# Projections of the token mixer: v made turned, low-rank halves side by side, log-gate product as one pass of stacked rows

## The reference

```python
(aq, ak, av, gq, gk, gv, gr, glf, glb, ga, gg) = split_cols(h @ p['w_in'][l])
attn = windowed_gqa(aq..., ak..., av..., p['attn_sink'][l])
...
la_f = log_sigmoid(glf @ p['gla_wa2_fwd'][l] + p['gla_ba_fwd'][l]) / 16
la_b = log_sigmoid(glb @ p['gla_wa2_bwd'][l] + p['gla_ba_bwd'][l]) / 16
```

## Time and profile before

| what | before |
|---|---|
| profiled execution | 3897.49 us |
| span | 3895.8 us |
| granted TensorE clock, mean of the span | 0.951 |
| TensorE busy | 3536.0 us (91%) |
| VectorE busy | 2169.3 us (56%) |
| ScalarE busy | 1593.3 us (41%) |
| GpSimd busy | 651.0 us (17%) |

### The profile page before, as it was taken

How to read it: one execution, slowest core, us unless ns; L and a number is a source line. 1 busy time by engine, 2 the same in 40 slices (tenths; PEclk the granted TensorE clock), 3 DMA queues, 4 the chain that set the end, 5 groups by cost and what they waited for, 6 DMA issues and landing times. The chain is left out here.

```text
span 3895.8 us, 56808 instructions
## 1 busy us (share of the span) xinstructions
PE 3536.0 (91%) x21432; PEld 2934.1 (75%) x21432; DVE 2169.3 (56%) x3920; ACT 1593.3 (41%) x2374; POOL 651.0 (17%) x709
## 2 busy tenths in 40 slices
PE   7699999998889999979999928999999999999991
PEld 3377777766667777757878728999999999999991
DVE  1344534554568888745545465565555555555555
ACT  1344545544334344334444303444444444443442
POOL 0010100101023443402322200011110001000005
PEclk9799999999999999989999858999999999999996
DMA  9733432421754554456555434555555555555567
GB/s 303 238 120 87 136 115 86 130 86 64 232 169 137 168 155 138 120 168 204 187 185 187 154 135 157 157 167 169 170 174 161 165 164 175 172 162 166 162 218 272
DMA packets 544843, 634.46 MB, mean 163 GB/s; under 512 B 77560, under 2 KB 431896, under 8 KB 543776
## 3 DMA queue, kind: packets, MB, share of 16 engines
q1 hardware_dynamic: 506960, 493.72, 40.4%
q0 software_dynamic: 35840, 123.75, 10.0%
q10 hardware_dynamic: 1872, 14.68, 0.9%
HBM read 505.20 MB, written 126.88 MB: 162 GB/s over the span
## 5 line engine op out<-in xcount | busy, mean ns | idle before, releaser
L2414 DVE TENSOR_TENSOR moe_w_lo<-moe_w_raw,moe_w_hi 128x2048 fp32r<-128x2048 f32 x192 | 439.9, 2291 | 371.5 <-ACT moe_w_hi L2362 338.5
L103 PE MATMUL moe_pg<-moe_x_hi,moe_w_hi 128*128 128x320 f32 x2048 | 635.5, 310 | 1.4 <-DVE moe_x_lo L2452 1.4
L104 PE MATMUL moe_pg<-moe_x_lo,moe_w_hi 128*128 128x320 f32 x2048 | 633.8, 309 | 0.0
L105 PE MATMUL moe_pg<-moe_x_hi,moe_w_lo 128*128 128x320 f32 x2048 | 633.8, 309 | 0.0
L2362 ACT CAST moe_w_hi<-moe_w_raw 128x2048 fp32r<-128x2048 f32 x192 | 364.9, 1900 | 158.2 <-DMA moe_w_raw<-in_w_gate_e_dram 81.2
L103 PEld LDWEIGHTS moe_pg<-moe_x_hi,moe_w_hi 128*128 128x128 f32 x2048 | 385.3, 188 | 2.4 <-issue 1.5
L104 PEld LDWEIGHTS moe_pg<-moe_x_lo,moe_w_hi 128*128 128x128 f32 x2048 | 385.4, 188 | 0.6
L105 PEld LDWEIGHTS moe_pg<-moe_x_hi,moe_w_lo 128*128 128x128 f32 x2048 | 385.3, 188 | 0.0
L103 PE MATMUL gla_pd<-gla_h_hi,gla_w_hi 128*128 128x512 f32 x640 | 261.1, 408 | 34.5 <-DVE gla_h_lo L1012 31.9
L103 PE MATMUL pa_pu<-pa_h_hi,pa_w_hi 128*128 128x512 f32 (+1 forms) x560 | 226.9, 405 | 37.4 <-DVE pa_h_lo L644 37.4
L105 PE MATMUL gla_pd<-gla_h_hi,gla_w_lo 128*128 128x512 f32 x640 | 252.4, 394 | 0.0
(11 more groups left out here) (326 smaller groups left out, 7664.0 us busy)
## 6 DMA issues: line engine op xcount, KB each, us to landing
moe_w_raw<-in_w_gate_e_dram SPq DMA_DIRECT2D x64, 1024.0 KB
moe_w_raw<-in_w_up_e_dram SPq DMA_DIRECT2D x64, 1024.0 KB
moe_w_raw<-in_w_down_e_dram SPq DMA_DIRECT2D x64, 1024.0 KB
gla_w_raw<-in_w_in_dram SPq DMA_DIRECT2D x80, 512.0 KB, 4.0
pa_w_raw<-in_w_in_dram SPq DMA_DIRECT2D x35, 1024.0 KB
front_w<-in_w_ada_dram SPq DMA_DIRECT2D x24, 1024.0 KB, 11.9
scratch_gate<-gla_sg POOLq DMA_DIRECT2D x80, 256.0 KB, 2.3
mix_sg<-scratch_gate SPq DMA_DIRECT2D x40, 512.0 KB, 4.6
```

The costliest lines, as they stand in the source:

```text
L103: pe.matmul(out, w_hi, x_hi, start=start, stop=False)
L104: pe.matmul(out, w_hi, x_lo, start=False, stop=False)
L105: return pe.matmul(out, w_lo, x_hi, start=False, stop=stop)
L2414: dve.tensor_tensor(w_lo[:, m % 2], w_raw[:, m % 2], w_hi[:, m % 2].bitcast(F32), ALU.subtract).then_inc(s_wlo, 1)
```

## The change

Three edits, all in `phase_proj_attn`.

1. Unit v is made as k is: its 128 weight columns are stationary and 512 tokens move. ScalarE copies the bank to `vT` (a part of `soft`). A new unit vt after q0 turns it back with four TensorE transposes, and ScalarE copies that bank to `v`.
2. Unit l has high and low weights side by side in `w_hi` as 64 stationary columns. One pass against the high activations gives both products, a second of 32 columns adds high weights x low activations: 16 matmuls instead of 24. The two 32-row halves of the bank are then added: ScalarE copies the one out, VectorE adds the other.
3. The la product is one float32r pass over 96 stacked rows. In `gl` they are high, low, high; in `wa2` high, high, low. ScalarE writes the two high copies, VectorE the low one. The weights are loaded three times (six DMAs instead of two) and split once.

The counts on the semaphore `s_evac` shift by these units (l no longer counts there, vt does), and the waits on the constants go from 80 to 144.

```diff
-BLOCK_UNITS = [("k", 0, 0), ("v", 0, 0), ("q", 0, 1), ("q", 1, 1), ...
+BLOCK_UNITS = [("k", 0, 0), ("v", 0, 0), ("q", 0, 1), ("vt", 0, None), ("q", 1, 1), ...
-ACT_KINDS = ("k", "v", "q", "l", "gq", "gk", "gv")
+ACT_KINDS = ("k", "v", "vt", "q", "gq", "gk", "gv")
...
-        gl = M.sb("gl", [2 * RANK, BLK])
-        wa2 = M.sb("wa2", [2 * RANK, 2, GLA_K])
+        gl = M.sb("gl", [P, BLK], F32R)
+        wa2 = M.sb("wa2", [P, 2, GLA_K], F32R)
+        vT, rank = soft[:, 0], (soft[0:2 * RANK, 1], soft[0:2 * RANK, 2])
+        wa_raw = soft[:, 3].rearrange("p (d n) -> p d n", d=2)
...
-                sp.dma_start(wa2[0:RANK, 0, :], I["gla_wa2_fwd"][0]).then_inc(s_c, 16)
-                sp.dma_start(wa2[RANK:2 * RANK, 1, :], I["gla_wa2_bwd"][0]).then_inc(s_c, 16)
+                for n in range(3):
+                    at = n * 2 * RANK
+                    sp.dma_start(wa_raw[at:at + RANK, 0, :], I["gla_wa2_fwd"][0]).then_inc(s_c, 16)
+                    sp.dma_start(wa_raw[at + RANK:at + 2 * RANK, 1, :], I["gla_wa2_bwd"][0]).then_inc(s_c, 16)
...
+                        wait(act, s_lat, b)
+                        act.copy(vT, bank[:]).then_inc(s_evac, 1)
+                    elif kind == "vt":
                         act.copy(v[:, b * TPB:(b + 1) * TPB].rearrange("p t n -> p (t n)"), bank[:]).then_inc(s_evac, 1)
...
-                        act.copy(gl[:], bank[0:2 * RANK, :]).then_inc(s_evac, 1)
+                        act.copy(rank[0], bank[2 * RANK:4 * RANK, :]).then_inc(s_g, 1)
+                        act.wait_ge(s_gs, b + 1)
+                        act.copy(gl[0:2 * RANK, :], rank[1])
+                        act.copy(gl[4 * RANK:6 * RANK, :], rank[1]).then_inc(s_ghi, 1)
...
+                act.copy(wa2[:], wa_raw).then_inc(s_wa, 1)
...
+                    low = w_hi[:, m % 2, :, n:2 * n] if CHUNKS[m % NCH] == "l" else w_lo[:, m % 2, :, 0:n]
...
-                dve.memset(wa2[:], 0.0).then_inc(s_z, 1)
+                dve.memset(wa_raw, 0.0).then_inc(s_z, 1)
...
+                dve.wait_ge(s_wa, 1)
+                lo = slice(4 * RANK, 6 * RANK)
+                dve.tensor_tensor(wa2[lo], wa_raw[lo], wa2[lo].bitcast(F32), ALU.subtract).then_inc(s_wa, 1)
...
+                        if kind == "l":
+                            dve.wait_ge(s_g, b + 1)
+                            dve.tensor_tensor(rank[1], pu[n % BANKS][0:2 * RANK, :], rank[0], ALU.add).then_inc(s_gs, 1)
+                            dve.wait_ge(s_ghi, b + 1)
+                            dve.tensor_tensor(gl[2 * RANK:4 * RANK, :], rank[1], gl[0:2 * RANK, :].bitcast(F32),
+                                              ALU.subtract).then_inc(s_glo, 1)
...
-                            pe.wait_ge(s_evac, evac_no(b, 6))
+                            pe.wait_ge(s_glo, b + 1)
                             if b == 0 and i == 0:
-                                pe.wait_ge(s_c, 80)
-                            mm = pe.matmul(bank[:], wa2[:, i // 2, i % 2 * P:(i % 2 + 1) * P], gl[:], start=True, stop=True)
+                                pe.wait_ge(s_wa, 2)
+                            rows = slice(0, 6 * RANK)
+                            mm = pe.matmul(bank[:], wa2[rows, i // 2, i % 2 * P:(i % 2 + 1) * P], gl[rows], start=True, stop=True)
+                        elif kind == "vt":
+                            pe.wait_ge(s_evac, evac_no(b, 1))
+                            for t in range(TPB):
+                                mm = pe.transpose(bank[:, t * P:(t + 1) * P], vT[:, t * P:(t + 1) * P], K.ident[:])
+                        elif kind == "l":
+                            s, m = c % 2, 2 * RANK
+                            for k in range(KD):
+                                if k == KD // 2 and (b, j) in MID:
+                                    step(MID[b, j])
+                                if k:
+                                    pe.matmul(bank[0:m, :], w_hi[:, s, k, 0:m], h_lo[:, k], start=False, stop=False)
+                                mm = pe.matmul(bank[0:2 * m, :], w_hi[:, s, k, 0:2 * m], h_hi[:, k], start=k == 0, stop=k == KD - 1)
+                                if k == 0:
+                                    pe.matmul(bank[0:m, :], w_hi[:, s, k, 0:m], h_lo[:, k], start=False, stop=False)
```

More of the change, by code:

```diff
@@ L361 @@
 CHUNKS = ["kv", "q01", "q23", "l", "gq", "gk", "gv0", "gv1", "gr01", "gr23"]
-BLOCK_UNITS = [("k", 0, 0), ("v", 0, 0), ("q", 0, 1), ("q", 1, 1), ("q", 2, 2), ("q", 3, 2), ("l", 0, 3),
+BLOCK_UNITS = [("k", 0, 0), ("v", 0, 0), ("q", 0, 1), ("vt", 0, None), ("q", 1, 1), ("q", 2, 2), ("q", 3, 2), ("l", 0, 3),
                ("gq", 0, 4), ("la", 0, None), ("gq", 1, 4), ("la", 1, None), ("gk", 0, 5), ("la", 2, None),
@@ L368 @@
 NU = len(BLOCK_UNITS)
-ACT_KINDS = ("k", "v", "q", "l", "gq", "gk", "gv")
+ACT_KINDS = ("k", "v", "vt", "q", "gq", "gk", "gv")
 N_ACT = sum(kind in ACT_KINDS for kind, _i, _c in BLOCK_UNITS)
 def attention_plan():
-    dense = [j for j, (kind, _i, _c) in enumerate(BLOCK_UNITS) if kind != "la"]
+    dense = [j for j, (kind, _i, _c) in enumerate(BLOCK_UNITS) if kind not in ("la", "vt")]
     mid, end = {}, {}
@@ L431, in phase_proj_attn @@
         s_c, s_z = M.sem("consts_loaded"), M.sem("wa2_zeroed")
+        s_wa, s_g = M.sem("wa2_split"), M.sem("rank_low_half")
+        s_gs, s_ghi, s_glo = M.sem("rank_sum"), M.sem("rank_hi"), M.sem("rank_lo")
         s_h = [M.sem(f"h_loaded{i}") for i in range(RING)]
@@ L608, in _ @@
                 split_w(1)
-                act.wait_ge(s_c, 80)
+                act.wait_ge(s_c, 144)
+                act.copy(wa2[:], wa_raw).then_inc(s_wa, 1)
                 for b in range(NB):
@@ L636, in split_w @@
                     n = width(m)
-                    dve.tensor_tensor(w_lo[:, m % 2, :, 0:n], w_raw[:, m % 2, :, 0:n],
+                    low = w_hi[:, m % 2, :, n:2 * n] if CHUNKS[m % NCH] == "l" else w_lo[:, m % 2, :, 0:n]
+                    dve.tensor_tensor(low, w_raw[:, m % 2, :, 0:n],
                                       w_hi[:, m % 2, :, 0:n].bitcast(F32), ALU.subtract).then_inc(s_wlo, 1)
@@ L655, in tables @@
                     ins.then_inc(s_bias, 1)
-                    dve.wait_ge(s_c, 80)
+                    dve.wait_ge(s_c, 144)
                     dve.tensor_scalar(nsink[:].rearrange("p g n -> p n g"), sink[:].rearrange("p (n g) -> p n g", n=KV), -1.0,
@@ L794, in bank_free @@
                     kind, i, _c = BLOCK_UNITS[j]
-                    if kind == "la":
+                    if kind == "l":
+                        pe.wait_ge(s_gs, b + 1)
+                    elif kind == "la":
                         pe.wait_ge(s_min, 4 * b + i + 1)
@@ L804, in scores @@
                     if g == 0:
-                        pe.wait_ge(s_evac, (t + hi - 2) // TPB * N_ACT + 6)
+                        pe.wait_ge(s_evac, (t + hi - 2) // TPB * N_ACT + 7)
                     wait(pe, s_s, x)
@@ L851, in _ @@
                         if kind == "la":
-                            pe.wait_ge(s_evac, evac_no(b, 6))
+                            pe.wait_ge(s_glo, b + 1)
                             if b == 0 and i == 0:
-                                pe.wait_ge(s_c, 80)
-                            mm = pe.matmul(bank[:], wa2[:, i // 2, i % 2 * P:(i % 2 + 1) * P], gl[:], start=True, stop=True)
-                        elif kind in ("v", "gv"):
+                                pe.wait_ge(s_wa, 2)
[15 more added lines that the diff above has]
+                                    pe.matmul(bank[0:m, :], w_hi[:, s, k, 0:m], h_lo[:, k], start=False, stop=False)
+                        elif kind == "gv":
                             s = c % 2
-                            tiles = range(TPB) if kind == "v" else range(i % 2 * 2, i % 2 * 2 + 2)
-                            cs, nc_ = (slice(P, 2 * P), P) if kind == "v" else (slice(0, 256), 256)
+                            tiles = range(i % 2 * 2, i % 2 * 2 + 2)
+                            cs, nc_ = slice(0, 256), 256
                             for r, t in enumerate(tiles):
@@ L868, in _ @@
                             s = c % 2
-                            m = 2 * RANK if kind == "l" else P
-                            cs = slice(i % 2 * P, i % 2 * P + m)
+                            col = 1 if kind == "v" else i % 2
+                            cs = slice(col * P, (col + 1) * P)
                             for k in range(KD):
@@ L875, in _ @@
                                     step(MID[b, j])
-                                mm = product3(pe, bank[0:m, :], w_hi[:, s, k, cs], w_lo[:, s, k, cs], h_hi[:, k],
+                                mm = product3(pe, bank[:], w_hi[:, s, k, cs], w_lo[:, s, k, cs], h_hi[:, k],
                                               h_lo[:, k], k == 0, k == KD - 1)
```

## The result

The kernel after takes 3851.4 us (median of four runs, 3846.1 to 3854.0), the one before on the same chip 3900.4 (median of four, 3892.9 to 3907.7): a ratio of 0.9871, interval 0.9849 to 0.9892. The forecast was 3857, in a range of 3844 to 3878.

The account below looks back on a forecast made before the run. PE's own instruction list was taken to bound the stage, nothing else being near full. 23.7 + 6.4 + 16.4 - 1.9 = 44.6 us, off 3901.6, gave 3857 us, range 3844 to 3878.

Parts of the forecast that it names:

- v, with vt: Projection units: v's 96 narrow matmuls become 24, saving 26.0 us over five blocks; added transposes cost 2.3; net 23.7.
- l, waits taken off: Low-rank unit: 24 matmuls become 16, saving 9.2 us; new waits take 0.7 and 2.1 back, leaving 6.4.
- la: Log-gate products, 20 units: two records of 1.05 us become one pass of 0.23, saving 16.4; other bound 12.8.
- SP's queue: Stage start: four more small weight DMAs at 0.47 delay block 0's h piece, costing 1.9 us; bounds nothing and 4.6.
- vt's price: Four added transposes per block: 0.45 us taken, bounds 0.35 and 0.60; 2.3 in five blocks.
- the 0.2 taken for block 1: Block 1's gq0: a 0.2 us wait for the gq weight split, beside about 0.5 in block 0.
- the other bound: Log-gate products: from a record's length of 0.41 us where nothing overlaps, 0.64 saved each, 12.8 in all.
- Width changes: Rival 1, unit l: each of 14 width changes costs, 6.3 to 11 us in all; about 3865 us; 17%.
- The rule that was weighed: Unit l: a change of tiling mode, as between 64 and 32 columns, drains TensorE; taken as the first rival.
- The stacked product: Rival 2, la: the product still takes two records, so 16.4 us are lost; 3874 us; 5%.
- l's hand-over: Rival 3, unit l: ACT and DVE waiting on each other become the bound; 3 us a leg gives 3907; 3%.
- the base of the forecast: Time of the kernel before from which 44.6 us was taken: 3901.6, the middle of all four times shown.

Follow-up runs that it names:

- la alone: Only the stacked log-gate product, with six weight DMAs, on the kernel before: stage 773.8 us; with block 0's last h piece loaded first, 753.2 and 3869.4 us in all.
- l alone: Only the low-rank unit with 16 matmuls on the kernel before, log-gate product left plain float32 in two records: stage 773.3 us, 7.4 less.
- the last experiment: Kernel after with block 0's last h piece issued first, plus DVE scores between l's addition and subtraction: 3836.8 us, ratio 0.9838 to before.
- v alone: Only the turned v with vt added, on the kernel before: stage 758.2 us, 22.5 less.
- before again: The kernel before, unchanged, run for a second profile: 3911.8 us, stage 791.7 us.

## Why the prediction was right

The forecast had the mechanism, the sign and the place: PE's list was shortened, and the end moved by what the list lost, less the waits that took its place. By its steps, in us of the stage, each measured on PE over its own stretch of all five blocks:

| step | forecast | measured |
|---|---|---|
| v, with vt (from k to l, without PE's waits) | -23.7 | -23.8 (222.6 to 198.8) |
| l, waits taken off (from l to gq0, and block 4's wait) | -6.4 | -6.5 (36.0 to 26.9, less waits of 0.48, 0.42 and 1.71) |
| la (from gq0 to the next k, without PE's waits) | -16.4 | -19.8 (508.0 to 488.2; la alone has the same) |
| waits for h: SP's queue in block 0 | +1.9 | +2.75 (10.61 for 7.86), and 0.2 at other block starts |
| sum | -44.6 | -47.1, which is the stage's |

**v** came as worked out from the distance of 512-column starts. vt's price was 0.35 at the least and 0.45 as taken, and it measured 0.36 with 0.32 to the next start, so 0.45 in all.

**l** is the step with the most at stake, and its chain was read right: in block 4 PE stands 0.42 us behind the shorter l (l alone has that wait too) and 1.71 behind the hand-over of DVE and ACT, where 0.5 and 1.6 were worked out. Here is that chain on DVE of after (addition, subtraction, then the row maxima that PE waits for), and PE's wait at the end of it:

```profile
798.26 0.67 DVE L736 TENSOR_TENSOR pa_soft<-pa_pu,pa_soft 32x512 f32<-32x512 f32 x1
...
800.25 0.68 DVE L738 TENSOR_TENSOR pa_gl<-pa_soft,pa_gl 32x512 fp32r<-32x512 f32 x1 [1.32 <-ACT pa_gl L591]
800.96 0.56 DVE L682 CUSTOM_DVE_ANT_0 pa_sc<-pa_p_s,pa_bias 128x384 f32<-128x384 f32 x1
```

```profile
802.06 0.92 PE L835 MATMUL pa_p_s<-pa_kT,pa_q 64*128 64x384 f32 x4 [1.71 <-DVE pa_mx L682]
```

That the order on DVE causes the 1.71 was tested, by the last experiment. In blocks 1 to 3 nothing waits, as forecast; the 0.2 taken for block 1 did not come.

**la** is the term that was mis-sized, 19.8 for 16.4. The prediction said "A saving above 16.4 I exclude, since no dense matmul of 512 columns is shorter." That held for la's own interval (0.31 is left of 1.05, so it saves 0.74, not 0.82), but left out the neighbours: around block 2's first la the transposes ahead lose 0.18 and the unit behind 0.11. The bound was set on the instruction, where it should have been set on the stretch between two units that don't change. (The 0.41 of the other bound is no length without overlap: it is the mean length of records that overlap.) PE's busy time in the stage, said to fall by about 46, fell by 52.7; the prediction's own list, before any wait, makes 23.7 + 9.2 + 16.4 = 49.3, so its 46 was too low by its own sum too.

**SP's queue** came out above its price, inside its bounds: each of the four added loads was priced at 0.47, the row of one. The first small load in the queue of before (to set against the earlier trace rows), and the queue of after:

```profile
179.53 1.15 SPq L511 DMA_DIRECT2D pa_wa<-in_gla_wa_fwd_dram  x1
```

```profile
177.95 1.14 SPq L517 DMA_DIRECT2D pa_soft<-in_gla_wa_fwd_dram  x1
...
180.06 1.54 SPq L518 DMA_DIRECT2D pa_soft<-in_gla_wa_bwd_dram  x1
...
182.11 0.42 SPq L518 DMA_DIRECT2D pa_soft<-in_gla_wa_bwd_dram  x1
...
187.63 1.13 SPq L507 DMA_DIRECT2D pa_h_raw<-scratch_hT  x1
```

Four of the six take 0.42 or 0.43, but one 1.14 and one 1.54, and the piece of h that PE waits for stands at the end of the same queue: from the first of these loads to that piece it is 9.68 us, in before 7.14. The 2.75 is of one pair of profiles, though. PE goes on with that piece 13.9 to 14.6 us after the stage's start in the four profiles with two loads and 15.9 to 16.6 in the five with six, so between the means the step is 2.1, near the forecast.

**The rivals.** Width changes cost nothing that can be seen: 3.79 us for 16 starts is 0.237 each, 5.65 for 24 was 0.235. The rule that was weighed, the Trainium skill, "TensorEngine Tiling (Array Packing)", Key Properties, is not borne out for 64 and 32 columns in float32r. For rows there is a price: among instructions of 128 rows the 32-row form of la costs 0.39 more than 96 rows, and part of it falls on the transposes ahead. Whether that price is a drain no run shows. The stacked product is one record, and l's hand-over takes 1.7 us, in block 4 alone, not 8.9 a block.

**What was not seen at all** is that before had two lengths of block 0. The profiled execution of before, from which the sum was made, has the short one; runs of 3907 to 3914 us are likely to have the long one (of those runs one, of 3911.8, was profiled, and shows it; for the others it is argued). The stages of the two profiles of before differ by 11.0 us, the middles of the two groups by 11.2. Of five profiles of kernels with the turned v and waits of 8.7 to 10.9 us, all have the clock at 1.00 from 204 us on; of four with the narrow v and waits of 6.9 to 10 us, two stayed low for the whole of v. So part of what the medians show, 49.1 against the stage's 47.1, can be of this kind. Why the clock rises in one execution of the same program and not in the other is open. That the base of the forecast, 3901.6, lay so near the measured 3900.4 is luck in part: three of the four runs under either are the same, and both are middles of two runs from each group, where no run of before lies (none on record between 3899.7 and 3903.9).

**The rest** of the program, span less stage, is 3115.1 in before and 3110.7 in after. Over all thirteen profiles it runs from 3110.7 to 3118.4, without order between kernels (after 3110.7, v alone 3112.1, before again 3118.4), so these 4 us are scatter. Of the 5.6 us by which the time came out below 3857, 2.5 are the stage's, 1.2 the base's, and 2 are this scatter or the clock of block 0.

## What to carry to other kernels

Where one in-order engine is full, price an edit by the distance from the last start that doesn't change to the next one that doesn't: the neighbours of a changed instruction pay too. A load that an engine stands for should be issued ahead of small transfers that are needed later. When times of a kernel fall in two groups, profile one execution of each before a gain of a few us is summed from either.

## What the runs showed of the hardware

- The granted clock can stay at 0.50 for 20 us in which PE has no gap (narrow v: 96 matmuls in 20.38 us in place of 10.7 to 11.0), and in another execution of the same program it rises at the start of that work. Where the wait ahead was 0.8 or 1.9 us, v took 10.66 and 10.67 us.
- A product of 32 rows among work of 128 rows costs 0.39 us more than one of 96 (block 2's first la; 7.1 us over 20), and plain float32 of 96 rows 0.63 more than float32r (12.6 over 20), both partly in the instructions around it.
- Sixteen float32r matmuls (512 moving columns) that alternate 64 and 32 stationary columns start 0.237 us apart, 24 of one width 0.235.
